# Down projection: fetching a row pair of two columns by row instead of by column

## The chip, the cores and the metric

The kernel runs on one core of one Trainium2 chip. The metric is device time in microseconds (us), the median of several executions. One further execution was profiled, and its trace is what the rows below show. Engines are TensorE (PE in the rows), VectorE (DVE), ScalarE (ACT), GpSimd (POOL) and SyncE (SP). SP does no arithmetic here: it waits on semaphores and issues DMAs.

## The reference

One decoder layer on 256 positions of width 2048: a norm, an input projection, three mixers side by side (gated linear attention, mLSTM, spatial gating), an output projection with the residual, then a SwiGLU feed-forward layer and a final norm. What the change touches is the last product:

```python
hf = rms_norm(x, norm_ffn)
gate, up = jnp.split(hf @ w_gu, 2, axis=-1)
return x + (jax.nn.silu(gate) * up) @ w_down      # [256, 5632] @ [5632, 2048], float32
```

## The kernel before

Every matrix product is made in a split form: an fp32 weight tile in `raw` is rounded by ScalarE into `w_hi` (`down_high`, L682), VectorE subtracts to get the rest into `w_lo` (`down_low`, L1269), and TensorE makes three products, hi by hi, lo by hi and hi by lo. A **unit** is one tile of 256 rows of the weight (two chunks of 128) by 512 columns: 512 KB. `raw`, `w_hi` and `w_lo` are rings of four slots (`R = 4`) each.

The down projection goes through the 2048 output columns in two halves of 1024, so each half has two columns of 512 (left and right). For each of 22 row pairs `k` (256 rows) the list `DOWN` holds one group:

- `pair`: the left unit and the right unit of row pair k, in two neighbouring `raw` slots q and q+1; 12 matmuls each.
- `seven`: the same two raw units, but multiplied in Strassen's way with seven products instead of eight. VectorE makes two further units of sums of the raw tiles (`weight_sums`, L1287, L1291 and L1293, which read both raw slots), ScalarE and VectorE split these too (L688, L1275), and TensorE does 6, 3, 6 and 6 matmuls for the four units. From the second raw slot only the second half is split.
- `left`, `right`: single units at the end of each half.

The first half runs pair k=1, pair k=3, then nine sevens (k = 0, 2, ... 16) with pairs k = 5, 7, ... 19 between them, then pair k=18 and four singles. The second half begins with seven k=0, alternates in the same way with pairs k = 1, 3, ... 15, and ends with pairs k=17 and k=18 and six singles. Of 44 row pairs 39 are thus fetched as a row pair of two columns, and 10 units singly. Since groups of two slots alternate in a ring of four, a seven and the pair behind it each keep their own two slots.

What sets the order of the work:

- SP issues the loads in the order of `DOWN`. The load of unit q waits until `w_lo` of the unit four before it in the ring (q - 4) is made, which is when its slot is free.
- ScalarE's `down_high` of a unit waits for its load, and for TensorE to have finished the unit four before it (`unit_used`). ScalarE and VectorE each work strictly in program order.
- VectorE's order inside a seven and the pair behind it: `weight_sums` (three operations), `down_low` of both raw units, `sum_low` twice, `down_low` twice for the pair.
- Near the start of the down projection GpSimd's queue brings back the residual (`x<-x_kept`, L430, two DMAs of 1 MB) and the row of the final norm (`nf_row`, L431, 1 MB). Between the halves VectorE folds the banks of the first half (`fold_banks`, `fold_sums`) and adds them to the residual (`down_add`, L1257), and TensorE waits for two of these adds before it uses their banks again.

Of the kernel before, what the change touches and what calls it, by code (L numbers as in the profile page):

```python
# [21 lines left out]
P = 128  # L22
# [14 lines left out]
GW = 512  # L37
UC = 2
R = 4
# [18 lines left out]
U_DN = U_FF + NG_FF * 2 * UPG  # L58
# [7 lines left out]
V_DN = FF_BASE + FF_SLOTS * NG_FF  # L66
# [26 lines left out]
def down_order():  # L93
    out, q, v = [], U_DN, V_DN
    odd = [1, 3, 5, 7, 9, 11, 13, 15, 17, 19]
    for half in range(2):
        lead = odd[:2] if half == 0 else []
        between = odd[len(lead):len(lead) + SUMMED - 1]
        rest = sorted(set(range(UPD)) - set(range(0, 2 * SUMMED, 2)) - set(lead) - set(between))
        groups = [("pair", k) for k in lead]  # L100
        for i in range(SUMMED):
            groups.append(("seven", 2 * i))
            if i < SUMMED - 1:
                groups.append(("pair", between[i]))
        alone = (2, LAST)[half]
        groups += [("pair", k) for k in rest[:-alone]]
        groups += [("left", k) for k in rest[-alone:]] + [("right", k) for k in rest[-alone:]]
        for kind, k in groups:
            out.append((kind, half, k, q, v))
            q += 2 if kind in ("pair", "seven") else 1  # L110
            v += {"pair": 2, "seven": 4}.get(kind, 1)
    return out, v


DOWN, V_END = down_order()


SLOT_OF = {}
for _kind, _half, _k, _q, _v in DOWN:
    SLOT_OF[_q] = _v  # L120
    if _kind in ("pair", "seven"):
        SLOT_OF[_q + 1] = _v + 1
LAST_SEVEN = [max(i for i, d in enumerate(DOWN) if d[0] == "seven" and d[1] == h) for h in range(2)]
FIRST_RIGHT = [i for i, d in enumerate(DOWN) if d[1] == 1][0]
SPLIT = [(0, 5), (5, 7), (7, SUMMED)]
# [5 lines left out]
def hybrid_layer(nc, x, norm_mix, w_in, gla_a2, gla_ab, gla_norm, ml_conv, ml_ib, ml_fb, ml_norm,  # L131
                 sgu_ln_g, sgu_ln_b, sgu_w, sgu_b, w_out, norm_ffn, w_gu, w_down, norm_final, out):
    ctx = ExitStack()
    with ctx:
# [5 lines left out]
        def sem(name):  # L140
            if name not in sems:
                sems[name] = ctx.enter_context(nc.semaphore(name))
            return sems[name]
# [24 lines left out]
        raw = sb("raw", [P, R, UC * GW], align=1024)  # L168
# [94 lines left out]
        loaded = [sem(f"w_loaded{s}") for s in range(R)]  # L263
        hi_ready, lo_ready, unit_used = sem("w_hi_ready"), sem("w_lo_ready"), sem("unit_used")

        def weights(w, row0, c0, width):
            return w[row0:row0 + UC * P, bass.ds(c0, width)].rearrange("(k p) n -> p k n", p=P)
# [4 lines left out]
        @block.sync  # L272
        def _(sp):
            def load(w, u, slot, row0, c0, width, first=False):
                if not first:
                    sp.wait_ge(lo_ready, u - R + 1)
                sp.dma_start(raw[:, slot, 0:UC * width].rearrange("p (k n) -> p k n", k=UC),
                             weights(w, row0, c0, width)).then_inc(loaded[slot], 16)


            def load_x(b, part):
                c0, width = X_PARTS[part]
                sp.dma_start(xin[:, b, c0:c0 + width],
                             x[b * P:(b + 1) * P, c0:c0 + width]).then_inc(sem(f"x_loaded{b}{part}"), 16)

            load_x(0, 0)
            sp.dma_start(rowsN[:, :], norm_mix.rearrange("(c p) -> c p", p=P)).then_inc(sem("norm_loaded"), 16)
            for u in range(U_OUT):
                for part in X_AHEAD.get(u, ()):
                    for b in range(NB):  # L290
                        load_x(b, part)
                c0, width, _at = IN_GROUPS[u // UPG]
                load(w_in, u, u % R, (u % UPG) * UC * P, c0, width, first=u < R)
            u = U_OUT
            for n, k in OUT_ORDER:
                load(w_out, u, u % R, k * UC * P, n * GW, GW)
                u += 1
            for k in range(2 * UPG):
                load(w_gu, U_FF + k, k % R, (k % UPG) * UC * P, FF if k >= UPG else 0, GW)

            def load_ff(j, k, i, up):
                sp.wait_ge(lo_ready, j * FF_SLOTS + (FF_BASE + FF_SLOT_OF[i] + 1))
                sp.dma_start(raw[:, i % R, :].rearrange("p (k n) -> p k n", k=UC),
                             weights(w_gu, k * UC * P, j * GW + (FF if up else 0), GW)).then_inc(loaded[i % R], 16)

            for j in range(1, NG_FF):
                for kind, k, i, _v in FF_ORDER:
                    if kind == "seven":
                        load_ff(j, k, i, False)
                        load_ff(j, k, i + 1, True)  # L310
                    else:
                        load_ff(j, k, i, kind == "up")

            def load_down(n, k, q):
                sp.wait_ge(lo_ready, SLOT_OF.get(q - R, V_DN + q - R - U_DN) + 1)
                sp.dma_start(raw[:, q % R, :].rearrange("p (k n) -> p k n", k=UC),
                             weights(w_down, k * UC * P, n * GW, GW)).then_inc(loaded[q % R], 16)

            for kind, half, k, q, _v in DOWN:
                if kind in ("pair", "seven"):  # L320
                    load_down(2 * half, k, q)
                    load_down(2 * half + 1, k, q + 1)
                else:
                    load_down(2 * half + (kind == "right"), k, q)
            def store(b, q):
                sp.dma_start(out[b * P:(b + 1) * P, q * GW:(q + 1) * GW],
                             x1[:, b, q * GW:(q + 1) * GW]).then_inc(sem("y_stored"), 16)

            for q in range(2):
                sp.wait_ge(sem("y0_by_dve"), q + 1)  # L330
                store(0, q)
            for q in range(2):
                sp.wait_ge(sem("y0_by_act"), q + 1)
                store(0, 2 + q)
            sp.wait_ge(sem("y1_by_dve"), 1)
            store(1, 0)
            sp.wait_ge(sem("y1_by_act"), 1)
            store(1, 2)
            sp.wait_ge(sem("y1_by_dve"), 2)
            store(1, 1)  # L340
            sp.wait_ge(sem("y_stored"), 16 * 4 * NB)
# [97 lines left out]
        def _(act):  # L439
# [237 lines left out]

            def down_high(v, q, c0=0):

                act.wait_ge(loaded[q % R], 16 * (q // R + 1))  # L680
                act.wait_ge(unit_used, v - R + 1)
                act.activation(w_hi[:, v % R, c0:UC * GW], raw[:, q % R, c0:UC * GW], ACT.Copy).then_inc(hi_ready, 1)  # L682

# [50 lines left out]
        def _(dve):  # L734
            chain = [0]

            def step(ins):

                chain[0] += 1
                ins.then_inc(sem("dve_chain"), 1)  # L740
# [109 lines left out]
            for u in range(UPG, U_FF):  # L850
# [83 lines left out]
                if u in CONV_AT:  # L934
                    dve.wait_ge(sem("ml_q_raw"), 1)
                    dve.wait_ge(sem("ml_k_raw"), 1)
                    pair = [(c, (qT if c < H else kT)[:, c % H, :]) for c in (2 * CONV_AT.index(u), 2 * CONV_AT.index(u) + 1)]
# [71 lines left out]
                if u == AT_SC + 3:  # L1009
# [3 lines left out]
                    for s, src in ((scA[:, :, :], mx[:, 2:4, :].rearrange("p k n -> p (k n)")), (scB[:, :, :], mx[:, 1, :])):  # L1013
                        s = s.rearrange("p h t -> p (h t)")
# [263 lines left out]
            def weight_sums(q, made, earlier):  # L1278

                a = q % R  # L1280
                if earlier is None:
                    dve.wait_ge(sem("act_ready"), 2 * NG_FF)
                else:
                    dve.wait_ge(lo_ready, earlier + 4)
                dve.wait_ge(loaded[a], 16 * (q // R + 1))
                dve.wait_ge(loaded[a + 1], 16 * (q // R + 1))
                dve.tensor_tensor(gate_s[:, :, :], raw[:, a + 1, :].rearrange("p (k n) -> p k n", k=UC),  # L1287
                                  raw[:, a:a + 2, 0:GW], ALU.subtract).then_inc(sem("w_sums"), 1)
                dve.wait_ge(sem("actT_psum"), NG_FF)
                dve.wait_ge(sem("w_sums"), made - 1)  # L1290
                step(dve.tensor_tensor(act_tok[:, 0, :], raw[:, a + 1, GW:2 * GW], gate_s[:, 0, :], ALU.subtract))  # L1291
                settle()
                dve.tensor_tensor(act_tok[:, 1, :], raw[:, a, GW:2 * GW], act_tok[:, 0, :], ALU.subtract)\  # L1293
                   .then_inc(sem("w_sums"), 1)
# [37 lines left out]
            for i, (kind, half, k, q, v) in enumerate(DOWN):  # L1332
# [22 lines left out]
                if i == 1:  # L1355
                    weight_sums(q + 2, 2, None)
                    act_low(NG_FF, 4 * (NG_FF - 1))
                after = i - LAST_SEVEN[half]
                if after == 2:
                    fold_banks(half, DOWN[LAST_SEVEN[half]][4] + 4)  # L1360
                if after == 3:
# [25 lines left out]
        def _(pe):  # L1387
# [394 lines left out]
            for i, (kind, half, k, q, v) in enumerate(DOWN):  # L1782
                final = kind in ("left", "right") and k == UPD - 1
                if kind == "seven":
                    down_seven(v, k, half, i == LAST_SEVEN[half], i in (2, FIRST_RIGHT))
                if kind in ("pair", "left"):
# [47 lines left out]
```

## Time and profile before

| | |
|---|---|
| median of three executions | 1103.69 us (1103.66 to 1104.41) |
| profiled execution, its own time | 1104.13 us |
| its span, first to last instruction | 1102.4 us |
| TensorE busy | 1090.8 us (99%) |
| VectorE busy | 863.6 us (78%) |
| ScalarE busy | 580.9 us (53%) |
| down projection, about | 857 to 1090 us of the span |

The span leaves out 1.7 us of launch and end that the device time contains. Times in the rows count from the start of the span. In rows with a name and `[0.5 <-X]` the engine stood idle for 0.5 us until X released it.

### The profile page before, as it was taken

How to read it: one execution, taken by the hardware profiler on the slowest of the kernel's cores; microseconds unless marked ns; L12 is line 12 of the kernel's file. 1: busy time of each engine (PE TensorE's matmuls, PEld its weight loads, DVE VectorE, ACT ScalarE, POOL GpSimd, SP SyncE). 2: the span in 40 equal slices, each digit the busy share in tenths (PEclk: the TensorE clock that was granted, in tenths of full speed). 3: DMA queues.
4: the chain of work that ended last, by engine and by line, in shares of the span. 5: the costliest groups of instructions: out<-in, count | busy, mean ns of one | idle time of the engine just before them, and what ended most of it. 6: DMA issues, size and time to landing. Idle time of an engine off the chain costs nothing.

```text
span 1102.4 us, 13887 instructions
## 1 busy us (share of the span) xinstructions
PE 1090.8 (99%) x5097; PEld 907.1 (82%) x5097; DVE 863.6 (78%) x1059; ACT 580.9 (53%) x704; POOL 41.3 (4%) x68
## 2 busy tenths in 40 slices
PE   9999999999999999999999999999999999999997
PEld 7797889888888888888888888888888888888885
DVE  5556866688756557988988889889888899899896
ACT  5655545555545444645545545446455556546553
POOL 2600000000010000000000000000000000000000
PEclk9999999999999999999999999999999999999999
DMA  8665646565546575656557557566566766666663
GB/s 283 212 201 171 179 134 180 160 172 153 187 176 224 178 263 175 211 170 213 197 162 230 165 177 241 173 194 209 170 212 194 282 206 213 199 199 210 201 224 115
DMA packets 110925, 215.31 MB, mean 195 GB/s; under 512 B 6940, under 2 KB 11616, under 8 KB 109984
## 3 DMA queue, kind: packets, MB, share of 16 engines
q1 hardware_dynamic: 108960, 205.36, 59.3%
q0 software_dynamic: 1632, 8.96, 2.2%
q8 instruction: 28, 0.46, 0.2%
q10 hardware_dynamic: 288, 0.39, 0.1%
q14 instruction: 17, 0.14, 0.0%
HBM read 210.49 MB, written 4.19 MB: 195 GB/s over the span
## 4 chain that ended last, share of the span: by engine, by line
PE 96%; DVE 2%; issue 1%; DMA 1%; ACT 0%; SPq 0%; POOLq 0%; POOL 0%; ACTq 0%; DVEq 0%
PE acc L1398 11%; PE acc L1400 11%; PE acc L1399 11%; PE acc L1669 11%; PE acc L1670 11%; PE acc L1671 11%; PE acc L1734 5%; PE acc L1735 5%; PE acc L1736 5%; PE mx L1390 2%; PE mx L1669 2%; PE mx L1670 2%; PE mx L1671 2%; PE mx L1734 1%; PE mx L1735 1%; PE mx L1736 1%
## 5 line engine op out<-in xcount | busy, mean ns | idle before, releaser
L749 DVE TENSOR_TENSOR w_lo<-raw,w_hi 128x1024 fp32r<-128x1024 f32 (+2 forms) x144 | 166.5, 1168 | 119.0 <-ACT w_hi L450 118.3
L450 ACT ACTIVATE w_hi<-raw 128x1024 fp32r<-128x1024 f32 (+2 forms) x144 | 144.5, 1014 | 136.1 <-PE acc L1400 130.9
L638 ACT ACTIVATE w_hi<-raw 128x1024 fp32r<-128x1024 f32 (+1 forms) x160 | 158.5, 1005 | 96.2 <-PE acc L1671 78.6
L1669 PE MATMUL acc<-w_hi,hT_hi 128*128 128x512 f32 x520 | 203.4, 391 | 0.0
L1169 DVE TENSOR_TENSOR w_lo<-raw,w_hi 128x1024 fp32r<-128x1024 f32 (+1 forms) x160 | 180.6, 1155 | 29.0 <-ACT w_hi L638 27.2
L1670 PE MATMUL acc<-w_lo,hT_hi 128*128 128x512 f32 x520 | 202.4, 389 | 0.0
L1671 PE MATMUL acc<-w_hi,hT_lo 128*128 128x512 f32 x520 | 202.3, 389 | 0.0
L1398 PE MATMUL acc<-w_hi,hT_hi 128*128 128x512 f32 (+2 forms) x444 | 169.1, 381 | 0.4 <-DVE w_lo L749 0.4
L1400 PE MATMUL acc<-w_hi,hT_lo 128*128 128x512 f32 (+2 forms) x444 | 166.4, 375 | 0.0
L1399 PE MATMUL acc<-w_lo,hT_hi 128*128 128x512 f32 (+2 forms) x444 | 166.3, 375 | 0.0
L1671 PEld LDWEIGHTS acc<-w_hi,hT_lo 128*128 128x128 f32 x520 | 97.6, 188 | 20.5
L1669 PEld LDWEIGHTS acc<-w_hi,hT_hi 128*128 128x128 f32 x520 | 97.6, 188 | 20.1
L1670 PEld LDWEIGHTS acc<-w_lo,hT_hi 128*128 128x128 f32 x520 | 97.7, 188 | 20.0
L682 ACT ACTIVATE w_hi<-raw 128x1024 fp32r<-128x1024 f32 x88 | 83.2, 969 | 34.1 <-PE acc L1736 25.5
L1269 DVE TENSOR_TENSOR w_lo<-raw,w_hi 128x1024 fp32r<-128x1024 f32 x88 | 94.5, 1111 | 6.0 <-ACT w_hi L682 3.9
L1736 PE MATMUL acc<-w_hi,actT_lo 128*128 128x512 f32 x250 | 97.3, 389 | 0.0
L1398 PEld LDWEIGHTS acc<-w_hi,hT_hi 128*128 128x128 f32 x444 | 83.4, 188 | 16.1 <-issue 0.9
L1400 PEld LDWEIGHTS acc<-w_hi,hT_lo 128*128 128x128 f32 x444 | 83.4, 188 | 15.2
L1399 PEld LDWEIGHTS acc<-w_lo,hT_hi 128*128 128x128 f32 x444 | 83.4, 188 | 14.0
L1734 PE MATMUL acc<-w_hi,actT_hi 128*128 128x512 f32 x232 | 90.5, 390 | 0.0
L1735 PE MATMUL acc<-w_lo,actT_hi 128*128 128x512 f32 x232 | 90.3, 389 | 0.0
L644 ACT ACTIVATE w_hi<-ff_sum 128x1024 fp32r<-128x1024 f32 x40 | 42.5, 1063 | 74.6 <-PE acc L1671 59.6
(296 smaller groups left out, 1512.5 us busy)
## 6 DMA issues: line engine op xcount, KB each, us to landing
raw<-in_w_gu SPq DMA_DIRECT2D x176, 512.0 KB, 4.1
raw<-in_w_down SPq DMA_DIRECT2D x88, 512.0 KB, 4.6
raw<-in_w_in SPq DMA_DIRECT2D x80, 512.0 KB, 3.9
raw<-in_w_out SPq DMA_DIRECT2D x32, 512.0 KB, 4.2
raw<-in_w_in SPq DMA_DIRECT2D x8, 272.0 KB, 2.9
raw<-in_w_in SPq DMA_DIRECT2D x8, 264.0 KB, 2.8
x<-in_x POOLq DMA_DIRECT2D x2, 1024.0 KB, 7.5
x_kept<-x POOLq DMA_DIRECT2D x2, 1024.0 KB, 6.5
```

The costliest lines, as they stand in the source:

```text
L638: act.activation(w_hi[:, v % R, c0:UC * GW], raw[:, i % R, c0:UC * GW], ACT.Copy).then_inc(hi_ready, 1)
L749: dve.tensor_tensor(w_lo[:, slot, 0:UC * width], raw[:, slot, 0:UC * width], w_hi[:, slot, 0:UC * width].bitcast(F32), ALU.subtract).then_ ...
L1169: dve.tensor_tensor(w_lo[:, v % R, c0:UC * GW], raw[:, i % R, c0:UC * GW], w_hi[:, v % R, c0:UC * GW].bitcast(F32), ALU.subtract).then_inc ...
L1398: pe.matmul(o, hi[:, c + i, tb], wh, start=first and i == 0, stop=False)
L1399: pe.matmul(o, hi[:, c + i, tb], wl, start=False, stop=False)
L1400: ins = pe.matmul(o, lo[:, c + i, tb], wh, start=False, stop=last and i == UC - 1)
L1669: pe.matmul(o, a[0], w[0], start=first, stop=False)
L1670: pe.matmul(o, a[0], w[1], start=False, stop=False)
L1671: return pe.matmul(o, a[1], w[0], start=False, stop=last)
L1734: pe.matmul(o, a[0], w[0], start=first, stop=False)
L1735: pe.matmul(o, a[0], w[1], start=False, stop=False)
L1736: return pe.matmul(o, a[1], w[0], start=False, stop=last)
```

## The change

The two units of a row pair are contiguous in `w_down`: 1024 neighbouring columns. Before, the left unit (256 rows by 512 columns) and the right unit were one DMA each. After, the first DMA brings rows 0 to 127 of both units (128 rows by 1024 columns) and the second brings rows 128 to 255 of both. Each still writes 512 KB, as runs of 2 KB in `raw`. A unit is complete only when both DMAs have landed, so both count on one semaphore (`pair_loaded0` or `pair_loaded2`, 32 for a pair), and both are issued behind one wait: that for `w_lo` of q + 1 - 4, the later of the two slots. Single units keep their DMA.

```diff
+LOADS = {}
+_count = {}
+for _kind, _half, _k, _q, _v in DOWN:
+    _name = f"pair_loaded{_q % R}" if _kind in ("pair", "seven") else f"single_loaded{_q % R}"
+    _count[_name] = _count.get(_name, 0) + (32 if _kind in ("pair", "seven") else 16)
+    LOADS[_q] = (_name, _count[_name])
+    if _kind in ("pair", "seven"):
+        LOADS[_q + 1] = LOADS[_q]
...
             def load_down(n, k, q):
                 sp.wait_ge(lo_ready, SLOT_OF.get(q - R, V_DN + q - R - U_DN) + 1)
                 sp.dma_start(raw[:, q % R, :].rearrange("p (k n) -> p k n", k=UC),
-                             weights(w_down, k * UC * P, n * GW, GW)).then_inc(loaded[q % R], 16)
+                             weights(w_down, k * UC * P, n * GW, GW)).then_inc(sem(LOADS[q][0]), 16)
+
+            def load_pair(n, k, q):
+                sp.wait_ge(lo_ready, SLOT_OF.get(q + 1 - R, V_DN + q + 1 - R - U_DN) + 1)
+                for r in range(UC):
+                    sp.dma_start(raw[:, q % R:q % R + 2, r * GW:(r + 1) * GW],
+                                 w_down[(UC * k + r) * P:(UC * k + r + 1) * P, n * GW:(n + 2) * GW]
+                                 .rearrange("p (s n) -> p s n", s=2)).then_inc(sem(LOADS[q][0]), 16)
 
             for kind, half, k, q, _v in DOWN:
                 if kind in ("pair", "seven"):
-                    load_down(2 * half, k, q)
-                    load_down(2 * half + 1, k, q + 1)
+                    load_pair(2 * half, k, q)
...
             def down_high(v, q, c0=0):
 
-                act.wait_ge(loaded[q % R], 16 * (q // R + 1))
+                act.wait_ge(sem(LOADS[q][0]), LOADS[q][1])
...
-                dve.wait_ge(loaded[a], 16 * (q // R + 1))
-                dve.wait_ge(loaded[a + 1], 16 * (q // R + 1))
+                dve.wait_ge(sem(LOADS[q][0]), LOADS[q][1])
```

On SP, where the down projection's loads stand between those of the gate and up weights and the stores of the result, the order before has one row for all 88 loads, each with its own wait:

```order
L277 DMA raw<-in_w_out 128x2x512 [waits w_lo_ready] x32
L277 DMA raw<-in_w_gu 128x2x512 [waits w_lo_ready] x16
L303 DMA raw<-in_w_gu 128x2x512 [waits w_lo_ready] x160
L316 DMA raw<-in_w_down 128x2x512 [waits w_lo_ready] x88
L326 DMA y<-x 128x512 [waits y0_by_dve] x2
```

The order of the change, at the passage from the first half to the second: the end of the last pair of the first half, its four single units, and the first seven and the first pair of the second half.

```order
L330 DMA raw<-in_w_down 128x2x512 [waits w_lo_ready]
L330 DMA raw<-in_w_down 128x2x512
L324 DMA raw<-in_w_down 128x2x512 [waits w_lo_ready] x4
L330 DMA raw<-in_w_down 128x2x512 [waits w_lo_ready]
L330 DMA raw<-in_w_down 128x2x512
```

The second DMA of a row pair (L330 without a wait) no longer has a wait of its own; the first carries the one that the second had.

On VectorE at the same passage, before (`weight_sums` is L1287 to L1293, `down_low` L1269, `down_add` L1257, `sum_low` L1275):

```order
L1269 TENSOR_TENSOR w_lo<-raw,w_hi 128x1024 [waits w_hi_ready,dve_chain]
L1269 TENSOR_TENSOR w_lo<-raw,w_hi 128x1024 [waits w_hi_ready]
L1287 TENSOR_TENSOR gate_s<-raw 128x1024 [waits w_loaded1,w_loaded0,w_lo_ready]
L1291 TENSOR_TENSOR act_tok<-raw,gate_s 128x512 [waits w_sums,actT_psum]
L1293 TENSOR_TENSOR act_tok<-raw,act_tok 128x512 [waits dve_chain]
L1269 TENSOR_TENSOR w_lo<-raw,w_hi 128x1024 [waits w_hi_ready]
L1257 TENSOR_TENSOR x<-acc,x 128x512 [waits unit_used] x2
L1269 TENSOR_TENSOR w_lo<-raw,w_hi 128x512 [waits w_hi_ready]
L1275 TENSOR_TENSOR w_lo<-gate_s,w_hi 128x1024 [waits w_hi_ready]
L1257 TENSOR_TENSOR x<-acc,x 128x512 [waits unit_used] x2
```

and after:

```order
L1283 TENSOR_TENSOR w_lo<-raw,w_hi 128x1024 [waits w_hi_ready,dve_chain]
L1283 TENSOR_TENSOR w_lo<-raw,w_hi 128x1024 [waits w_hi_ready]
L1300 TENSOR_TENSOR gate_s<-raw 128x1024 [waits pair_loaded0,w_lo_ready]
L1304 TENSOR_TENSOR act_tok<-raw,gate_s 128x512 [waits w_sums,actT_psum]
L1306 TENSOR_TENSOR act_tok<-raw,act_tok 128x512 [waits dve_chain]
L1283 TENSOR_TENSOR w_lo<-raw,w_hi 128x1024 [waits w_hi_ready]
```

No arithmetic has moved on any engine; only what the waits stand for has.

## Rows read from the trace of the kernel before

**Rows 1.** Page, part 1: busy time, share of the span, instructions.
```profile
PE 1090.8 (99%) x5097; PEld 907.1 (82%) x5097; DVE 863.6 (78%) x1059; ACT 580.9 (53%) x704; POOL 41.3 (4%) x68
```

**Rows 2.** Waits of TensorE, 850 to 1102 us: total us, times, longest.
```profile
PE acc L1734 <- DVE x L1257: 0.3, 1, 0.3
```

**Rows 3.** Waits of VectorE, same stretch.
```profile
DVE w_lo L1275 <- ACT w_hi L688: 11.8, 14, 0.9
...
DVE gate_s L1287 <- DMA raw<-in_w_down: 1.2, 3, 0.5
```

**Rows 4.** One period (seven and pair) by windows; columns as in the header.
```profile
core 0: us, PE busy (x) PEld busy (x) DVE busy (x) ACT busy (x) POOL busy (x), PEclk, DMA share, GB/s
...
950.20:960.40 10.20, 10.20 (x46) 8.45 (x45) 8.98 (x10) 5.83 (x6) 0.00 (x0) 1.00 0.62 202
```

**Rows 5.** Timeline of VectorE, the same period: start, length, line.
```profile
947.82 1.22 DVE L1275 TENSOR_TENSOR w_lo<-gate_s,w_hi 128x1024 fp32r<-128x1024 f32 x1
949.98 1.23 DVE L1275 TENSOR_TENSOR w_lo<-act_tok,w_hi 128x1024 fp32r<-128x1024 f32 x1 [0.95 <-ACT w_hi L688]
951.35 2.36 DVE L1269 TENSOR_TENSOR w_lo<-raw,w_hi 128x1024 fp32r<-128x1024 f32 x2
953.63 1.22 DVE L1287 TENSOR_TENSOR gate_s<-raw 128x1024 f32<-128x1024 f32 x1
...
956.28 1.82 DVE L1269 TENSOR_TENSOR w_lo<-raw,w_hi 128x1024 fp32r<-128x1024 f32 x2
```

**Rows 6.** Tile raw on SP, 897.3 to 898.2 us: a seven's two loads.
```profile
L316 SPq DMA_DIRECT2D raw<-in_w_down x2: 368/368/368, 897.3 to 897.9; - x2
...
DMA to landing us min/median/max: 4.2/4.5/4.9
```

**Rows 7.** Tile raw on SP, 970.0 to 970.3 us: one load alone.
```profile
L316 SPq DMA_DIRECT2D raw<-in_w_down x1: 368/368/368, 970.0 to 970.0; - x1
...
DMA to landing us min/median/max: 3.6/3.6/3.6
```

**Rows 8.** DMA queues, 878.5 to 880 us: packets, MB, share.
```profile
q1 hardware_dynamic: 248, 0.48, 93.8%
```

**Rows 9.** Page, part 6: DMAs of 1 MB, median us to landing.
```profile
x<-x_kept POOLq DMA_DIRECT2D x2, 1024.0 KB, 8.6
```

**Rows 10.** Timeline of VectorE, seven k=6 of the first half.
```profile
902.91 1.23 DVE L1287 TENSOR_TENSOR gate_s<-raw 128x1024 f32<-128x1024 f32 x1 [0.38 <-DMA raw<-in_w_down]
...
909.01 1.23 DVE L1275 TENSOR_TENSOR w_lo<-act_tok,w_hi 128x1024 fp32r<-128x1024 f32 x1 [0.48 <-ACT w_hi L688]
```

**Rows 11.** Tile raw on SP, 868.8 to 869 us: right unit of pair k=5.
```profile
L316 SPq DMA_DIRECT2D raw<-in_w_down x1: 367/367/367, 868.9 to 868.9; - x1
...
DMA to landing us min/median/max: 10.3/10.3/10.3
```

**Rows 12.** DMA queues, 872 to 877 us.
```profile
q0 software_dynamic: 225, 1.65, 78.4%
q1 hardware_dynamic: 214, 0.43, 22.2%
```

**Rows 13.** Timeline of ScalarE, pair k=5.
```profile
878.57 2.01 ACT L682 ACTIVATE w_hi<-raw 128x1024 fp32r<-128x1024 f32 x2 [0.30 <-PE acc L1736]
```

**Rows 14.** Timeline of VectorE, pair k=5.
```profile
879.66 2.36 DVE L1269 TENSOR_TENSOR w_lo<-raw,w_hi 128x1024 fp32r<-128x1024 f32 x2
```

**Rows 15.** Timeline of TensorE: last matmul of the seven, first of pair k=5.
```profile
880.80 0.39 PE L1736 MATMUL mx<-w_hi,actT_hi 128*128 128x512 f32 x1
881.03 0.39 PE L1734 MATMUL acc<-w_hi,actT_hi 128*128 128x512 f32 x1
```

**Rows 16.** Timeline of VectorE, between the halves.
```profile
974.14 1.22 DVE L1287 TENSOR_TENSOR gate_s<-raw 128x1024 f32<-128x1024 f32 x1
...
980.86 1.28 DVE L1257 TENSOR_TENSOR x<-acc,x 128x512 f32<-128x512 f32 x2
```

**Rows 17.** Timeline of TensorE, between the halves.
```profile
981.69 0.47 PE L1734 MATMUL acc<-w_hi,s_hi 128*128 128x512 f32 x1 [0.26 <-DVE x L1257]
```

## The prediction

> **What bounds the kernel now.** I read first the busy times of the page: TensorE is busy for 99% of the span [rows 1]. The reader is to see that nothing can be gained here that does not take idle time from TensorE. Then TensorE's waits in the down projection: one wait of 0.3 us in 250 us [rows 2]. So this change can hardly make the kernel faster, and the question is whether it makes TensorE wait. The third view is one period of the alternation (a seven and the pair behind it): 10.20 us, TensorE busy all of it, VectorE 8.98 us [rows 4]. VectorE has 1.2 us to spare per period, of which 0.95 us stand in one place, before the second sum unit, where it waits for ScalarE and through it for TensorE [rows 5]. Over the whole down projection VectorE waits 11.8 us there in 14 times, and only 1.2 us in 3 times for weights [rows 3]. A delay of VectorE up to about 0.95 us in a period is therefore given back in the same period; one that falls where there is no such gap goes on to TensorE.
>
> **What the change costs, part by part.**
>
> *Fewer and later issues.* Both DMAs of a row pair leave when the later of the two slots is free, 0.37 us apart (the length of one issue [rows 6]). For a seven the first load now leaves 0.6 us later (897.3 to 897.9), since its two slots come free 0.6 us apart; for a pair it leaves 1.1 us later, the time of one `down_low` (2.36 us for two [rows 5]). The second DMA leaves 0.37 us later than the right unit's did. Nothing queues on SP behind it but the next loads, which come microseconds later.
>
> *When is a row pair complete?* Both units need both DMAs, 1 MB. No row of before shows this, so I bound it. A load alone lands 3.6 us after its issue [rows 7]. When the queue has work it moves 248 packets in 1.5 us [rows 8], so the 256 packets of a second load take 1.55 us: at least 3.6 + 1.55 = 5.15 us, unless the landing of the first hides part of it. From above: the two loads of a seven, 0.6 us apart, are both down 0.6 + 4.9 = 5.5 us after the first issue [rows 6]. I take 5.2 us, since with 0.37 us between the issues the first bound is nearest. The far upper bound is the 1 MB DMA at 8.6 us [rows 9], but that is the median of two beside other traffic.
>
> The Trainium skill (DMA: Bandwidth & Descriptors, Anatomy of one DMA) gives 2.0 us plus bytes over 436 GB/s, fitted to GpSimd's path. By it 512 KB would take 3.2 us where the row has 3.6, and 1 MB would take 4.4 us; the lone load here is slower than the rule, so I keep the rows. With 4.4 us the place between the halves below would cost 0.3 us instead of 1.1.
>
> *The steady sevens: nothing.* A seven's slots are both free when its half-width `down_low` ends, just as the sum unit of 947.82 begins [rows 5], so both loads leave at 947.9 and are down by 947.9 + 5.2 = 953.1, at most 953.4. VectorE wants them at 953.63 [rows 5]. ScalarE gets the left unit later than now, but `down_low` needs it only at 956.28 [rows 5], three microseconds on. What hides the cost is VectorE's own row of two sum units, one wait and two `down_low`, 5.7 us long. For the pair, the loads leave when its two `down_low` end (951.35 + 2.36 = 953.7 [rows 5]) and are down by 959. VectorE comes to them one period of 10.2 us after 951.35, at 961.55, and ScalarE 1.1 us before that (as at 878.57 and 879.66 [rows 13, 14]), at 960.45: 1.4 us to spare. If a landing is later than 5.7 us, the 0.95 us gap takes the next part, so the margin is 6.7 us before a period grows.
>
> *The early sevens of the first half: nothing, with little to spare.* There VectorE already waits for the weights, 0.38 us at 902.91 [rows 10]. The loads leave at 897.9, so 903.1 to 903.4 instead of 897.9 + 4.9 = 902.8: 0.3 to 0.6 us more. In the same period VectorE has a gap of 0.48 us before the second sum unit [rows 10]. I take 0, with up to 0.3 us in the range. The same for the seven two periods on.
>
> *Pair k=5 of the first half: +1.9 us.* This is the one place where loads meet other traffic. The right unit's load, issued at 868.9, takes 10.3 us and lands at 879.2 [rows 11], because GpSimd's queue q0 is bringing back the residual and the norm row: from 872 to 877 us q0 moves 1.65 MB and q1 only 0.43 MB [rows 12]. The left unit left SP when the slot before came free, ahead of all that traffic. Now half of each unit is in the second DMA, and the first is no longer ahead either: 1 MB has to come through where 0.5 MB did. The packets of the second load come behind those of the first: 879.2 + 1.55 = 880.75; I take off 0.15 because the left unit's packets are gone from the start of that stretch. So 880.6. ScalarE began the left unit at 878.57 [rows 13]; now it begins at 880.6, 2.05 us later. VectorE follows in step: its `down_low` began 1.09 us after ScalarE and ran 1.22 us, to 880.88 [rows 14], and TensorE's first matmul of the pair began at 881.03, right behind the seven's last [rows 15]. So the slack was 0.15 us, and TensorE waits 2.05 - 0.15 = 1.9 us. Lower bound: the pair lands with the first DMA at 879.2, 879.2 - 878.57 - 0.15 = 0.5 us. Upper bound: the second load is served at half speed beside q0's tail, another 1.55 us, 3.4 us. The next seven's loads are behind in the same queue, but VectorE reaches their sums 2 us later too, so they cost nothing more.
>
> The Trainium skill (DMA: Bandwidth & Descriptors, Queues, rings and completion order) says that each DMA engine takes turns between the queues it has work for, a packet at a time. The trace agrees: 225 packets of q0 and 214 of q1 in the same 5 us, with 7.3 KB in each of q0 and 2 KB in each of q1. By it the second load's packets would, while q0 lasts, come only one for each large packet of the other, which speaks for the upper side.
>
> *The first seven of the second half: +1.1 us.* Its left unit was loaded some microseconds ahead; its right unit left at 970.0, when the slot of the second single came free, and that load alone landed at 973.6 [rows 7], and VectorE began the sums at 974.14 without a wait [rows 16]. Now both leave at 970.0 and are down at 975.2: VectorE starts 1.1 us later. Here nothing gives it back: from the folding of the banks on, VectorE is busy without a gap until the adds into the residual at 980.86 [rows 16], and for one of these TensorE waits already, 0.26 us at 981.69 [rows 17]. The whole 1.1 us reaches TensorE. Bounds from 5.15 and 5.5 us: 1.0 to 1.4; if the pair's first load finds the queue empty and the second overlaps it fully, 0.3.
>
> *The end.* The last pair k=18 completes later by up to 1 us, but VectorE stands some microseconds ahead of TensorE there, and the singles are unchanged: 0.
>
> **The sum.** 0 + 0 + 1.9 + 1.1 = 3.0 us. On the profiled execution's own time, 1104.13 + 3.0 = 1107.1 us; the median of the runs is 0.44 us under that execution, so 1103.69 + 3.0 = 1106.7 us, +0.27%.
>
> **The rivals.**
>
> 1. *Only one of the two waits appears.* If q0's tail and the seven's landing overlap so that the pair k=5 is complete at 879.2, the cost there is 0.5 us and the sum 1.6 us, 1105.3; if the place between the halves costs 0.3 us by the faster landing, the sum is 2.2 us or less. For it: the landing at 879.2 is that of the slowest DMA engines, and the others may have room for a second load before it. Against: the last of 16 engines decides, and it has 16 packets more. It decides against my forecast where the two costs together stay below 2.2 us. This ends on the other side, not slower by a measurable amount.
>
> 2. *The landing of 1 MB is slower than its two halves suggest.* If a row pair takes 7.2 us, nearer to the 8.6 us of rows 9, each of the 15 or so steady sevens is 0.5 us later than the 6.7 us margin: 7.5 us, plus 3.0, plus 2 us more in each of the two places: 14.5 us, about 1118. Against: every load of before is bandwidth and a fixed part, nothing suggests that two neighbouring runs of 2 KB cost more than two distant ones.
>
> 3. *The rows of 4 KB read faster than two of 2 KB.* Neighbouring columns are read together, so the second load might be nearly free, and both costs would go to 0.3 to 0.5 us: 1104.4. A gain beyond this has no idle time to come from: all of TensorE's waits together are 0.3 us [rows 2].
>
> **How the numbers follow.** A measurement of this kernel tells about 0.2%, 2.2 us, from no change. Forecast (both waits, 2.2 to 4.8 us): 58%, of which nearly all is slower. Rival 1: 20%, within 0.2%. Rival 2: 10%, slower. Rival 3: 9%, within 0.2%, with 2% in it for faster. The remaining 3% are slower for a reason not seen. Slower 0.69, same 0.29, faster 0.02. Low end: rival 3 at 1104.2. High end: both upper bounds, 3.4 + 1.4 + 0.3 + 0.3 = 5.4 us, 1109.1, and a little of rival 2: 1109.8.
>
> **What would show each step.** In the profile after: TensorE waits once for VectorE's `w_lo` near 881 to 883 us, about 1.9 us, behind ScalarE waiting for raw; and near 982 us for the add into x, about 1.4 us. The DMAs of the down projection show a longer median to landing, about 4.9 us. VectorE's wait before the second sum unit stays near 0.95 us in the later sevens and is shorter in the early ones. The prediction is wrong if TensorE waits inside the later alternation (rival 2), or if no wait for raw stands before pair k=5 (rival 1).

## The result, and the profile after

| | before | changed |
|---|---|---|
| median | 1103.82 us (10 runs, 1103.15 to 1105.77) | 1107.09 us (10 runs, 1106.14 to 1109.36) |
| profiled execution, span | 1102.4 us | 1105.8 us |

The ratio is 1.0028, 95% interval 1.0020 to 1.0037: slower by 3.3 us. The forecast was 1106.7 us. The sum was nearly right, but by luck: its larger term, 1.9 of 3.0 us, did not appear, and other losses stand in its place, as the profile shows.

The busy times of the changed kernel, page part 1, and the loads in part 6:

```profile
PE 1092.7 (99%) x5097; PEld 908.0 (82%) x5097; DVE 863.7 (78%) x1059; ACT 579.1 (52%) x704; POOL 41.3 (4%) x68
...
raw<-in_w_down SPq DMA_DIRECT2D x88, 512.0 KB, 4.7
```

Every engine has as many instructions as before [rows 1] and is busy for as long to within 2 us; what grew is waiting. The waits of TensorE in the down projection, 850 us to the end (engine, line, what it waited for: total, times, longest):

```profile
PE acc L1747 <- DVE x L1271: 1.8, 1, 1.8
PE acc L1747 <- DVE act_tok L1094: 0.3, 1, 0.3
PE mx L1747 <- DVE w_lo L1283: 0.2, 1, 0.2
```

Before there was one of 0.3 us [rows 2], for the same add into x as the first of these. VectorE, same stretch (the line of the sums of the weight tiles is now L1300, of the sum units L1289), and ScalarE:

```profile
DVE gate_s L1300 <- DMA raw<-in_w_down: 13.6, 14, 1.6
...
DVE w_lo L1289 <- ACT w_hi L702: 1.2, 3, 0.8
```

```profile
ACT w_hi L696 <- DMA raw<-in_w_down: 46.7, 23, 5.2
```

VectorE waited for weights 3 times, 1.2 us in all, and 11.8 us for ScalarE [rows 3]. Now the two have changed places: 14 of the 18 sevens wait for their weights, 0.6 to 1.6 us each, and the gap before the second sum unit, which was free time, has shrunk by as much. TensorE does not see this in the steady periods. But the free time is spent, as VectorE's rows of one period show:

```profile
946.40 1.23 DVE L1300 TENSOR_TENSOR gate_s<-raw 128x1024 f32<-128x1024 f32 x1 [1.01 <-DMA raw<-in_w_down]
...
949.07 1.82 DVE L1283 TENSOR_TENSOR w_lo<-raw,w_hi 128x1024 fp32r<-128x1024 f32 x2
...
956.66 1.22 DVE L1300 TENSOR_TENSOR gate_s<-raw 128x1024 f32<-128x1024 f32 x1 [1.07 <-DMA raw<-in_w_down]
```

From the start of the sums to the end of the two `down_low`, which frees the slots, are 4.5 us (946.40 to 950.9); from there to the landing of the next seven's two loads 5.65 us (to 956.57), and 0.1 us later the next sums begin. This circle takes 10.26 us, as long as TensorE's period of 10.20 us [rows 4]. A VectorE that is late therefore stays late: after a second load of 6.0 us in the second half (issued at 993.9) that seven and all six behind it wait 0.6 to 0.8 us each. Where the two loads are down a little sooner the lag shrinks slowly: in mid_col (experiment 1), with 5.5 us in the median, three sevens in a row wait 1.60, 0.68 and 0.39 us. Before, the later load was down 0.9 us ahead of VectorE in this period (952.74 against 953.63).

**Between the halves.** The two loads of the first seven of the second half leave SP at 972.0 and 972.4 and land 4.3 and 5.1 us later, so the row pair is complete 5.5 us after its first issue:

```profile
L330 SPq DMA_DIRECT2D raw<-in_w_down x2: 368/420/472, 972.0 to 972.4; - x2
...
DMA to landing us min/median/max: 4.3/4.7/5.1
```

VectorE there, and TensorE's first matmul behind the add:

```profile
973.78 2.36 DVE L1283 TENSOR_TENSOR w_lo<-raw,w_hi 128x1024 fp32r<-128x1024 f32 x2
977.59 1.22 DVE L1300 TENSOR_TENSOR gate_s<-raw 128x1024 f32<-128x1024 f32 x1 [1.45 <-DMA raw<-in_w_down]
...
984.33 1.28 DVE L1271 TENSOR_TENSOR x<-acc,x 128x512 f32<-128x512 f32 x2
```

```profile
985.16 0.47 PE L1747 MATMUL acc<-w_hi,s_hi 128*128 128x512 f32 x1 [1.80 <-DVE x L1271]
```

Before, VectorE began the sums at 974.14 without a wait and TensorE waited 0.26 us [rows 16, 17]. Now VectorE waits 1.45 us and TensorE 1.80 us: 1.54 us more, the whole of VectorE's delay.

**Pair k=5 of the first half**, where the forecast had its larger term. Its loads, and ScalarE taking it up:

```profile
L330 SPq DMA_DIRECT2D raw<-in_w_down x2: 367/438/509, 870.1 to 870.5; - x2
...
DMA to landing us min/median/max: 7.7/8.3/8.8
```

```profile
879.82 2.01 ACT L696 ACTIVATE w_hi<-raw 128x1024 fp32r<-128x1024 f32 x2 [0.30 <-PE acc L1749]
```

The pair is complete at 879.3, half a microsecond before ScalarE wants it, and ScalarE is released by TensorE as before [rows 13], not by the load. There is no wait of TensorE. The reason is GpSimd's last fetch, page part 6 of the changed kernel and then of the one before:

```profile
nf_row<-in_norm_final POOLq DMA_DIRECT2D x1, 1024.0 KB, 9.8
```

```profile
nf_row<-in_norm_final POOLq DMA_DIRECT2D x1, 1024.0 KB, 12.5
```

The left unit's load is no longer beside the start of GpSimd's queue. That queue is done 2.7 us sooner, and the pair has the DMA engines to itself that much earlier. The other traces of this document bear this out: `nf_row` takes 12.5 to 13.3 us in all seven kernels whose left unit of pair k=5 leaves ahead of GpSimd's fetches, and 9.5 to 9.8 us in all six in which it leaves behind them (nf_late, experiment 11, moves this fetch). One of these six loads by column (late_col, below), so it is the time of the issue that counts and not the shape.

**Around 869 and 888 us** TensorE has two small waits that the sum had not counted:

```profile
869.00 0.50 PE L1747 MATMUL acc<-w_hi,actT_hi 128*128 128x512 f32 x1 [0.26 <-DVE act_tok L1094]
```

```profile
888.81 0.50 PE L1747 MATMUL mx<-w_hi,actT_hi 128*128 128x512 f32 x1 [0.25 <-DVE w_lo L1283]
```

The first begins with the load of the left unit of pair k=3. ScalarE takes it up 2.00 us after it fell idle, released by the load and no longer by TensorE, and VectorE, which works in order, brings the last activations (`act_tok`) late behind it. The rows are of ScalarE and of VectorE:

```profile
863.74 1.06 ACT L696 ACTIVATE w_hi<-raw 128x1024 fp32r<-128x1024 f32 x1 [2.00 <-DMA raw<-in_w_down]
```

```profile
864.84 1.23 DVE L1283 TENSOR_TENSOR w_lo<-raw,w_hi 128x1024 fp32r<-128x1024 f32 x1 [1.84 <-ACT w_hi L696]
...
868.19 0.75 DVE L1094 SCALAR_TENSOR_TENSOR act_tok<-up_s,stat,gate_s 128x512 f32<-128x512 f32 x1
```

The second is seven k=2, whose second load took 5.9 us after an issue at 878.9.

```profile
L330 SPq DMA_DIRECT2D raw<-in_w_down x2: 368/732/1097, 878.5 to 878.9; - x2
...
DMA to landing us min/median/max: 4.3/5.1/5.9
```

**A part that is not the change.** The two profiled executions differ by 3.44 us in span, but 0.95 us of it stand in the first 26 us, where both programs do the same. The windows of the first 26 us, before and after: TensorE has started 108 matmuls in the one and 103 in the other.

```profile
0.00:26.00 26.00, 23.28 (x108) 18.96 (x109) 12.70 (x19) 12.99 (x22) 7.82 (x20) 1.00 0.86 279
```

```profile
0.00:26.00 26.00, 23.58 (x103) 19.41 (x104) 12.64 (x19) 12.33 (x20) 7.78 (x20) 1.00 0.87 277
```

So I compare the start of the same matmul (the nth of 5097) in both traces, and count steps of the difference from there on. This table is used for all runs below; "mean" is the mean of all executions less that of the kernel before in the same session, with its standard error.

```
steps of TensorE's start against the profiled execution of before, us
                  to 26   26-880  880-900  900-975  975-990  990-1085   mean of executions
change            +0.95   +0.31   +0.58    +0.09    +1.52     0.00      +3.1 +- 0.4
mid_col           -0.02   +0.01   +0.52    +0.57     0.00    +0.73      +1.3 +- 0.3
mid_row_only      -0.27   -0.02   +0.33    -0.04    +1.30     0.00      +1.8 +- 0.3
late_col          -0.20   -0.01   +0.61    -0.06    +1.90     0.00      +2.2 +- 0.2
steady_row_only   -0.77   -0.19    0.00    -0.03     0.00     0.00      +0.9 +- 0.4
steady_again      -0.72   -0.21    0.00    -0.03     0.00    +0.34      +0.3 +- 0.2
col_again         -0.34   -0.16    0.00    -0.06    -0.01    +0.36      -0.1 +- 0.2
open_row_only     +0.59   +0.07   +0.59    -0.06    +0.01     0.00      +0.5 +- 0.2
pairs_row         -0.45   +0.57   +0.09    -0.03    -0.03     0.00      +0.6 +- 0.3
sevens_row        -0.34   -0.09   +0.66    -0.00    +0.01    +0.07      +0.3 +- 0.2
fold_later        -0.24   +0.06   +0.69    -0.05     0.00     0.00      +0.9 +- 0.3
before_fold_later -0.34   -0.06   +0.25    -0.03    -0.03     0.00       0.0 +- 0.2
nf_late           -0.16   -0.01   +0.41    +1.02    +1.23    +0.31      +3.3 +- 0.2
```

In the change 2.5 us of steps stand behind the first 26 us: 1.5 between the halves, 0.3 near 869, 0.6 near 888, 0.1 elsewhere. One profiled execution stands for each row, and steps of up to 0.36 us appear in kernels that have nothing by row at that place (near 888 before_fold_later and mid_row_only, behind 990 col_again), so only differences beyond that carry weight.

### The profile page after: what moved, and what is told of

Read it like the earlier page. It is cut to its first block, busy times and chain, and to the rows that moved or that the text cites. A ratio compares the mean times of both kernels' runs of the same rounds, so it can differ in the third digit from the quotient of the medians.

```text
span 1105.8 us, 13887 instructions
## 1 busy us (share of the span) xinstructions
PE 1092.7 (99%) x5097; PEld 908.0 (82%) x5097; DVE 863.7 (78%) x1059; ACT 579.1 (52%) x704; POOL 41.3 (4%) x68
## 4 chain that ended last, share of the span: by engine, by line
PE 92%; DVE 4%; DMA 2%; issue 1%; ACT 1%; SPq 0%; POOLq 0%; POOL 0%; DVEq 0%; ACTq 0%
PE acc L1411 11%; PE acc L1413 11%; PE acc L1412 11%; PE acc L1682 11%; PE acc L1684 11%; PE acc L1683 11%; PE acc L1747 4%; PE acc L1749 4%; PE acc L1748 4%; PE mx L1403 2%; PE mx L1682 2%; PE mx L1683 2%; PE mx L1684 2%; DMA raw<-in_w_down 1%; PE mx L1747 1%; PE mx L1749 1%
```

## The experiments

All but three kernels are the change with a choice of which groups are fetched by row, by a function `BY_ROW`. The others are fetched by column, each unit behind its own wait, as before:

```diff
+                    if BY_ROW(i, kind, half, k):
                         load_pair(2 * half, k, q)
+                    else:
+                        if LATE:
+                            sp.wait_ge(lo_ready, SLOT_OF.get(q + 1 - R, V_DN + q + 1 - R - U_DN) + 1)
+                        load_down(2 * half, k, q)
+                        load_down(2 * half + 1, k, q + 1)
```

**1. Undo the change at one seven (mid_col).**

```diff
+BY_ROW = lambda i, kind, half, k: not (half == 1 and kind == "seven" and k == 0)
```

> The change, but with the first seven of the second half fetched by column as before. Theory 1 (most of the loss is the late start of this one seven): TensorE's wait of 1.8 us for the add into x falls back to 0.3 us, so the time is 1.5 us under the change, about 1105.6 us. Theory 2 (the loss is spread over the many row pairs of the alternation): the time stays within 0.4 us of the change, about 1107 us.

Measured 1105.32 us, ratio 1.0009 (1.0000 to 1.0018). The step between the halves is gone. But theory 1 had this one place for all of the loss, and 1.3 us remain. In its profile TensorE waits three times for `w_lo`, near 888, 939 and 1064 us:

```profile
PE mx L1762 <- DVE w_lo L1296: 0.9, 3, 0.4
PE acc L1762 <- DVE x L1284: 0.3, 1, 0.3
```

The second is in the steady alternation of the first half, behind a second load that took 5.9 us instead of some 5.0 (rows of SP and of VectorE):

```profile
L337 SPq DMA_DIRECT2D raw<-in_w_down x2: 368/420/472, 929.1 to 929.5; - x2
...
DMA to landing us min/median/max: 3.9/4.9/5.9
```

```profile
935.44 1.22 DVE L1315 TENSOR_TENSOR gate_s<-raw 128x1024 f32<-128x1024 f32 x1 [1.60 <-DMA raw<-in_w_down]
```

This pair of loads was complete 6.2 us after its first issue. VectorE was already late there, with no gap left in the two periods ahead of it, so the new delay reached TensorE. The third is the largest step of this kernel (0.7 us), in the later alternation of the second half. There the second load of a seven, issued at 1052.6, took 7.0 us, so the pair of loads was complete after 7.5 us. VectorE was on time before it, and 0.7 us still reached TensorE; VectorE and TensorE:

```profile
1059.78 1.23 DVE L1315 TENSOR_TENSOR gate_s<-raw 128x1024 f32<-128x1024 f32 x1 [1.77 <-DMA raw<-in_w_down]
```

```profile
1063.71 0.50 PE L1762 MATMUL mx<-w_hi,actT_hi 128*128 128x512 f32 x1 [0.43 <-DVE w_lo L1296]
```

Late landings are not special to the fetching by row: in col_again (experiment 5), all by column, the two loads of a seven of the second half took 6.4 and 7.0 us, and TensorE's step there is the table's 0.36 us.

**2. The change at that one seven alone (mid_row_only).**

```diff
+BY_ROW = lambda i, kind, half, k: half == 1 and kind == "seven" and k == 0
```

> The kernel before, with only the first seven of the second half fetched by row. Theory 1: TensorE waits 1.8 us for the add into x, and the time is 1.5 us over before, about 1105.3 us. Theory 2: one seven of 39 row pairs costs under 0.3 us, 1103.9 us.

Measured 1105.30 us, 1.0018 (1.0008 to 1.0027). Theory 1: one of 39 row pairs brings +1.8 +- 0.3 us of mean, with 1.3 us of step there. TensorE:

```profile
PE acc L1762 <- DVE x L1284: 1.6, 1, 1.6
```

The means of experiments 1 and 2 add up to the change, 1.3 + 1.8 = 3.1 us, but each has an error of 0.3 us, and their steps behind the first 26 us (1.8 and 1.6 us) sum to more than the change's 2.5. That they agree to a tenth is chance.

**3. Late issue without the new shape (late_col).** All groups by column, `LATE = True`.

> The kernel before with its loads by column, one semaphore per unit, but both loads of every row pair issued behind the wait for the later slot, as in the change. Theory 1 (the later issue is what costs, not the shape of the DMAs): TensorE waits 1.5 to 1.8 us for the add into x, and the time is 2.5 to 3.5 us over before, 1106.3 to 1107.3 us. Rival (the joint completion of both units, or runs of 4 KB in the weight, cost): at most half of the change's loss, under 1105.5 us.

Measured 1105.84 us, 1.0019 (1.0010 to 1.0028). TensorE's wait for the add is 2.0 us; the steps behind the first 26 us sum to 2.45 us, those of the change to 2.49. The profile therefore shows the issue behind the later slot as the cause, and no cost of the rows of 4 KB or of the joint completion. Nor does the larger step between the halves speak for one (1.9 us against 1.5 in the change): it follows the landing. In the four kernels with this seven late, both its loads are down 5.2, 5.3, 5.5 and 5.9 us after the first issue, and the steps are 1.2, 1.3, 1.5 and 1.9 us (nf_late of experiment 11, mid_row_only, the change, late_col). The medians leave 1.0 us between the two kernels (2.2 +- 0.2 against 3.1 +- 0.4 of mean, in different sessions), and 1105.84 is under the 1106.3 that I had written down: a smaller share of joint completion is not excluded.

**4. Only the later groups by row (steady_row_only, and once more as steady_again).**

```diff
+BY_ROW = lambda i, kind, half, k: i >= 8 and not (half == 1 and kind == "seven" and k == 0)
```

The group with i = 8 is seven k=6 of the first half, so the groups to pair k=9 are by column; the first expectation names the limit as seven k=8, which is one group off.

> The change with the opening row pairs (up to seven k=8 of the first half) and the first seven of the second half fetched by column as before; all the others by row. Theory 1: no wait of TensorE beyond the 0.3 us of before, time within 0.4 us of before. Theory 2: 1 to 1.5 us over before.

> The kernel with only the later groups by row (from seven k=6 of the first half, without the first seven of the second half) once more. Its one profiled execution showed no new wait, but its eleven executions had a mean 0.95 us over those of before. If single late landings are what costs there, most executions lie within 0.3 us of before and some are 1 us or more over it, with a mean 0.3 to 1.2 us over; if the first time was chance, the mean is within 0.3 us.

Both profiles show only the 0.3 us wait of before, and no step of more than 0.34 us. The medians were 1105.05 us (1.0012, 1.0003 to 1.0021) and 1104.28 us (1.0004, 0.9995 to 1.0013); means +0.9 +- 0.4 and +0.3 +- 0.2. The first median lay 1.4 us over before, where theory 2 had it, and the second did not repeat this: the first was partly chance. That single late landings reach TensorE is what experiment 1 shows in one execution. The 0.34 us of steady_again, too, stand behind a seven whose second load took 6.7 us. How much they cost on average stays open.

**5. A control for the program around it (col_again).** All by column, own waits, but the semaphores of the change.

> A control: every row pair by column and behind its own wait, as before, but with the semaphores of the change (more of them, other names). If only the DMAs and their waits matter, it is the kernel before: within 0.3 us of it, with runs as close together as its are. If the extra semaphores or another layout of the program cost something in the first 40 us, its median is 0.5 us or more over before.

Measured 1103.92 us against 1104.13 us, 0.9998 (0.9989 to 1.0007). The additional semaphores and the other layout cost nothing; the 0.95 us in the first 26 us of the change's profile are chance, as the -0.77 to +0.59 us of the other kernels show.

**6. The opening alone (open_row_only).**

```diff
+BY_ROW = lambda i, kind, half, k: i < 8
```

> By row only the first eight groups of the down projection, to pair k=9 of the first half; all others by column. The profile of the change shows TensorE 0.3 us later near 869 us and 0.4 to 0.5 us later near 888 us than before, and no wait at pair k=5. If that comes from the fetching by row, this kernel shows the same two steps and is 0.5 to 0.9 us over before; the prediction on record would have it 1.9 us over.

Measured 1104.81 us, 1.0005 (0.9996 to 1.0014). The step near 888 is there (0.59), that near 869 is not (0.07 us in that column, against 0.31 in the change). Pair k=5, which is by row here, costs nothing; the 1.9 us of the prediction do not appear.

**7 and 8. Pairs alone, sevens alone (pairs_row, sevens_row).**

```diff
+BY_ROW = lambda i, kind, half, k: kind == "pair"
...
+BY_ROW = lambda i, kind, half, k: kind == "seven" and not (half == 1 and k == 0)
```

> By row only the 21 pairs, all sevens by column. A pair of the alternation has over 1 us to spare, so a late landing should not reach TensorE: the cost should be what stands in the opening, 0 to 0.8 us over before, and the spread of the runs as narrow as before.

> By row only the sevens, but not the first of the second half. A seven has 0.3 us to spare in the first half and some 1 us in the second, and a landing that is late by a microsecond or more, as single ones are, now holds back both units. Then this kernel should be 0.8 to 1.5 us over before, with a spread of 2 us or more between runs, like the change without the passage between the halves. If only the opening matters, it is within 0.5 us.

Measured 1104.76 us (1.0006, 0.9997 to 1.0015) and 1104.66 us (1.0005, 0.9996 to 1.0014). The step near 869 is in pairs_row (with the wait for `act_tok`, 0.3 us) and not in sevens_row, the one near 888 is in sevens_row (0.66) and not in pairs_row (0.09). Over all traces only the second is regular. Near 888 the seven kernels with seven k=2 issued late have 0.41 to 0.69 us and the six others 0 to 0.33. Near 869 the step comes only in the change and in pairs_row, where the second load of pair k=3 took 5.07 and 5.14 us to land; in the five others with this pair issued late it took 4.8 to 4.9 us, and there is no step beyond 0.07. The sevens by row cost less than expected, 0.3 +- 0.2 us, and their executions spread over 1.5 us, no more than before: the theory of the late landings is not borne out by this run.

**9 and 10. Free the slots before the folding (fold_later, before_fold_later).** VectorE makes `w_lo` of the second single, and with it frees the seven's second slot, before it folds the banks:

```diff
-                if after == 2:
+                if after == (3, 2)[half]:
                     fold_banks(half, DOWN[LAST_SEVEN[half]][4] + 4)
-                if after == 3:
+                if after == (4, 3)[half]:
                     fold_sums(half)
```

> The change, with VectorE's folding of the first half's banks moved behind the next single unit (fold_banks behind the second single, fold_sums behind the third). The slots of the first seven of the second half then come free some 4 us earlier. If the wait of 1.8 us comes from these slots coming free only behind the folding, it falls back to 0.5 us or less, and the time is 1.3 to 1.8 us under the change, about 1105.5 us. If it comes from the amount of work on VectorE there, which is the same, nothing changes: 1107 us.

> The kernel before with the same move of the folding. VectorE's work is what TensorE waits for there (0.3 us), not the load, so nothing is gained: within 0.4 us of before. If instead the folding moved back makes the adds into x late, it is up to 1 us slower.

With the change: 1104.75 us, 1.0009 (1.0000 to 1.0018). That is a mean 2.2 us under the change, more than the 1.3 to 1.8 expected, with an error of 0.5 (two sessions). The seven's loads leave at 966.7, not 972.0, and the second takes 5.5 us, not 5.1; VectorE starts the sums without a wait, and TensorE waits as in the kernel before:

```profile
L330 SPq DMA_DIRECT2D raw<-in_w_down x2: 368/420/472, 966.7 to 967.1; - x2
...
DMA to landing us min/median/max: 4.4/4.9/5.5
```

```profile
973.45 1.22 DVE L1283 TENSOR_TENSOR w_lo<-raw,w_hi 128x1024 fp32r<-128x1024 f32 x1
974.60 1.22 DVE L1300 TENSOR_TENSOR gate_s<-raw 128x1024 f32<-128x1024 f32 x1
```

```profile
982.15 0.47 PE L1747 MATMUL acc<-w_hi,s_hi 128*128 128x512 f32 x1 [0.26 <-DVE x L1271]
```

The step between the halves is 0.00 with VectorE's work unchanged. The loss there is that of a slot freed behind the folding. On the kernel before the same move changes nothing: 1103.70 us, 0.9998 (0.9989 to 1.0007). No kernel here beats the one before.

**11. Move GpSimd's 1 MB (nf_late).**

```diff
+            pool.wait_ge(unit_used, V_DN + 44)
             pool.dma_start(nf_row[:, :], norm_final.partition_broadcast(P)).then_inc(sem("nf_loaded"), 16)
```

> The change, with GpSimd's fetch of the norm row (1 MB) moved from the start of the down projection to the middle of its first half (some 90 us later). If the 0.5 us that TensorE loses near 888 us comes from traffic beside the loads of seven k=2, it falls to 0.1 us or less there, and seven k=2 lands within 5.6 us of its first issue instead of 6.3. If it comes from the later issue alone, the loss stays. Where the 1 MB now passes, a row pair should take 7 us or more and TensorE lose up to 2 us. Sum: within 2 us of the change.

Measured 1107.19 us, 1.0030 (1.0020 to 1.0041). The loss near 888 fell only to 0.41 us, not to 0.1, and seven k=2 was complete after 6.1 us, not within 5.6: most of this loss is not made by this fetch. Where the 1 MB passes now, the row pair beside it (pair k=19) takes 7.7 us for its second load (the first issue stands 0.4 us ahead), the seven behind it 6.7 us, and TensorE loses 1.0 us:

```profile
L330 SPq DMA_DIRECT2D raw<-in_w_down x2: 367/419/471, 943.9 to 944.3; - x2
...
DMA to landing us min/median/max: 4.4/6.1/7.7
```

```profile
954.38 0.50 PE L1748 MATMUL acc<-w_hi,actT_hi 128*128 128x512 f32 x1 [0.50 <-DVE w_lo L1284]
```

This is the price that the prediction had sought at pair k=5: 1 MB of other traffic beside a row pair does reach TensorE, here with 8.1 us from the first issue to completion, where the prediction had worked out 6.7 us as what a pair can hide.

## Why the prediction came out

- *The frame: right.* TensorE busy all the time, nothing to gain, a loss only where VectorE has no gap. Shown by the two waits having changed places in the steady periods at no cost to TensorE in the profile of the change.
- *Completion of a row pair, 5.2 us: under by 0.3 us.* It is 5.5 us in the place between the halves (0.4 + 5.1), the upper of the two bounds, and 5.2 to 5.9 us there in the other kernels with this seven late. The first of two loads does not land in the 3.6 us of a lone one [rows 7] but in 4.3; the second is 1.2 us behind.
- *Between the halves, +1.1 us: right in place and mechanism, short in size.* It is 1.5 us in the profile, 1.2 to 1.9 in other kernels with this seven late. The 0.3 us of completion are most of the difference; the other 0.1 us lie between the landing (977.50) and the start of the sums (977.59). Experiments 2 and 9 show it alone and gone.
- *Pair k=5, +1.9 us: the failed step.* It is "I take off 0.15 because the left unit's packets are gone from the start of that stretch". The load that is not there at the start gave GpSimd's queue, and so the pair behind it, more than the second load costs: the pair was complete 8.8 + 0.4 = 9.2 us after its first issue with 1 MB, where 0.5 MB took 10.3 us [rows 11]. TensorE is 1.3 us later there than before, so counted from TensorE the pair was complete at about 878.0 on the clock of before, and not at 880.6. The term is 0 and not 1.9 us. The prediction had named this as a sign of its being wrong (no wait for raw before pair k=5). Rival 1 comes nearest, but with 0.5 us left there and another reason.
- *The opening, taken at nothing: +0.3 and +0.6 us in this profile.* Pair k=3 does not stand in the prediction, nor that VectorE makes the last activations behind its `down_low`; experiments 7 and 8 show that this step comes only with a slow landing. Seven k=2 was put at nothing because VectorE would reach it 2 us later anyway, behind the wait at pair k=5; that wait never came. Of its 0.6 us up to 0.33 stand in kernels by column too.
- *The steady sevens at nothing: nearly, but for a wrong reason.* No step in the profile of the change, one of 0.34 us in experiment 4 with means of +0.3 and +0.9 us, and in experiment 1 two late landings that reached TensorE. The forecast that VectorE's gap of 0.95 us stays in the later sevens failed: it is 0.0 to 0.2 us in seven of the last eight. The margin of 6.7 us adds this gap to the 5.7 us of VectorE's row, which already contain it once. That holds for one late landing when VectorE is on time (mid_col: 7.5 us to completion, 0.7 us lost). If every landing is late, the gap is spent by the first, and the margin is 5.7 us; the change's sevens take 5.6 (median of those issued behind 888 us). By this estimate rival 2 would have cost about 1.5 us in each seven, not 0.5.

Rival 2 is out as a standing cost: in the change no row pair behind the opening takes more than 6.4 us. Single ones did take 7 us, in mid_col by row (7.5 us) as in col_again by column (7.6 us). Rival 3 is out by the 5.5 us. That 3.0 us were forecast and 3.3 measured is thus luck: the 3.3 are 1.5 us in a place that was seen rightly (at 1.1), 0.9 us that were not seen, and 0.8 us (3.3 - 2.5) that the profile of one execution does not show, in place of 1.9 us that never came. The mean of the change has an error of 0.4 us; how much of the 0.8 us is chance and how much late landings stays open.

The Trainium skill's price (DMA: Bandwidth & Descriptors, Anatomy of one DMA) would have made the pair complete after 4.4 us; the trace has 5.5 us, and the row decides. The Trainium skill's rule that DMA engines take turns between queues (the same page, Queues, rings and completion order) agrees with the last fetch of GpSimd, 9.8 us without our load beside its start and 12.5 us with it; these two times show that the queues share the engines, not how they take turns.

## What to carry to other kernels

Joining two tiles of a ring in one fetch makes both wait for the later slot and the later landing. Where the consumer's engine has a gap in each period, that costs nothing at first, but it spends the gap, and the next late landing finds none. Compare the whole circle (free a slot, load, use, free again) with the period of the engine that sets the pace. Then look for the one place where the slots are freed behind other work (here the folding between the halves), and free them first. When traffic is moved away from a busy stretch, work out what the other queue gains from it before charging anyone for the rest.

## What was not expected of the hardware

- Two loads of 512 KB issued 0.4 us apart land 4.1 to 4.5 and 5.0 to 5.4 us after their own issues in nearly all periods of the change, and both are down 5.6 us after the first issue (median of its sevens; 5.4 to 5.5 us in the other kernels with their sevens issued so). In the median the first takes 0.7 us more in the change than the 3.6 us of a lone one [rows 7], and 0.3 to 0.5 us more in the other kernels.
- Taking one load of 512 KB from the start of a stretch of 3 MB of GpSimd's traffic ended that traffic 2.7 us earlier (12.5 to 9.8 us for the last DMA), 1.7 times the 1.55 us that these packets take by themselves.
- The first 26 us, in which all these kernels do the same, differ by up to 1.7 us between executions (-0.77 to +0.95), which is half of the whole effect here: a single profile must be compared from behind that stretch.
